# Input and first weights in eight pieces by feature, the RMS factor applied at evacuation, and an output projection by feature, in a hybrid attention layer

## What is computed

```
xn = x * rsqrt(mean(x*x) + eps) * norm_g          # x: (544 tokens, 1024 features)
h  = xn @ w_in                                    # one projection, 6728 columns
qa, ka, va, ua, qi, ki, wi, qb, kb, vb, ub, ga, gb = split(h)
# A: indexer scores relu(qi . ki) weighted by wi, top-k keys, softmax attention (8 heads of 64)
# B: stick-breaking attention (8 heads of 64)
ya = (A * silu(ua)) @ w_a_out ; yb = (B * silu(ub)) @ w_b_out
y  = x + (sigmoid(ga) * ya + sigmoid(gb) * yb) @ w_o
# outputs: y, and the new rows of ka, va, ki, kb, vb for prompt and sample
```

## Time and profile before

| | us |
|---|---|
| median of 3 runs (lowest to highest) | 618.91 (618.16 to 620.35) |
| the profiled execution, its own time | 619.36 |
| its span, first to last instruction | 617.6 |
| PE busy in the span | 585.4 (95%) |
| DVE / ACT / POOL busy | 328.4 / 259.2 / 92.5 |
| share of PE in the chain that ended last | 90% |
| mean granted TensorE clock | 0.981 |

### The profile page before, as it was taken

How to read it: one execution, slowest core, us unless ns; L and a number is a source line. 1 busy time by engine, 2 the same in 40 slices (tenths; PEclk the granted TensorE clock), 3 DMA queues, 4 the chain that set the end, 5 groups by cost and what they waited for, 6 DMA issues and landing times.

```text
span 617.6 us, 10710 instructions
## 1 busy us (share of the span) xinstructions
PE 585.4 (95%) x4582; PEld 548.7 (89%) x4582; DVE 328.4 (53%) x619; ACT 259.2 (42%) x398; POOL 92.5 (15%) x82
## 2 busy tenths in 40 slices
PE   4699999999999999999989999995999999999998
PEld 3699999998887888878979898885999999999997
DVE  3614546688787786646764566447244322245331
ACT  5332545544587667740263455544122212213110
POOL 3701000300131325420600000150000000000000
PEclk9799999999999999998999999986999999999999
DMA  8532214062022020002542210210333322345411
GB/s 243 176 106 70 79 62 148 2 208 70 2 69 69 2 68 1 1 1 85 193 152 68 70 35 2 69 36 0 103 103 88 84 62 76 103 137 190 153 46 39
DMA packets 58176, 50.48 MB, mean 82 GB/s; under 512 B 4304, under 2 KB 53840, under 8 KB 58128
## 3 DMA queue, kind: packets, MB, share of 16 engines
q1 hardware_dynamic: 58128, 49.79, 26.2%
HBM read 42.82 MB, written 6.82 MB: 80 GB/s over the span
## 4 chain that ended last, share of the span: by engine, by line
PE 90%; ACT 4%; DVE 2%; DMA 1%; issue 1%; POOL 1%; SPq 0%; DVEq 0%; ACTq 0%
PE PS L518 36%; PE PS L789 15%; PE PS L840 8%; PE PS L857 7%; PE PS L502 3%; PE PS L668 3%; PE PS L610 3%; PE PS L640 2%; PE PS L580 2%; PE PS L723 2%; PE PS L767 2%; PE PS L746 1%; DMA tm<-in_x_prompt 1%; PE PS L645 1%; PE PS L861 1%
## 5 line engine op out<-in xcount | busy, mean ns | idle before, releaser
L1183 DVE TENSOR_TENSOR wlo<-raw,whi 128x2048 fp32r<-128x2048 f32 (+2 forms) x39 | 79.6, 2042 | 111.1 <-ACT whi L908 110.7
L518 PE MATMUL PS<-whi,xhi 128*128 128x256 f32 x384 | 110.6, 288 | 2.5 <-ACT q_flat L938 1.1
L518 PE MATMUL PS<-wlo,xhi 128*128 128x256 f32 x384 | 109.1, 284 | 0.0
L518 PE MATMUL PS<-whi,xlo 128*128 128x256 f32 x384 | 108.6, 283 | 0.0
L518 PEld LDWEIGHTS PS<-whi,xhi 128*128 128x128 f32 x384 | 73.1, 190 | 4.7 <-ACT q_flat L938 1.3
L789 PE MATMUL PS<-xhi,whi 128*128 128x272 f32 x256 | 74.6, 291 | 0.0
L789 PE MATMUL PS<-xlo,whi 128*128 128x272 f32 x256 | 74.5, 291 | 0.0
L789 PE MATMUL PS<-xhi,wlo 128*128 128x272 f32 x256 | 74.4, 290 | 0.0
L518 PEld LDWEIGHTS PS<-whi,xlo 128*128 128x128 f32 x384 | 73.3, 191 | 0.0
L518 PEld LDWEIGHTS PS<-wlo,xhi 128*128 128x128 f32 x384 | 72.9, 190 | 0.0
L518 PE MATMUL PS<-xhi,whi 128*128 128x272 f32 (+1 forms) x208 | 62.4, 300 | 4.8 <-POOL xlo L1622 3.4
(11 more groups left out here) (213 smaller groups left out, 1239.6 us busy)
## 6 DMA issues: line engine op xcount, KB each, us to landing
raw<-in_w_in SPq DMA_DIRECT2D x18, 1024.0 KB, 5.2
raw<-in_w_in SPq DMA_DIRECT2D x16, 512.0 KB, 4.5
raw<-in_w_o SPq DMA_DIRECT2D x4, 1024.0 KB, 6.2
tm<-in_x_prompt SPq DMA_DIRECT2D x4, 512.0 KB, 6.6
out<-vals SPq DMA_DIRECT2D x2, 1024.0 KB, 4.3
out<-tm SPq DMA_DIRECT2D x2, 1024.0 KB, 7.6
raw<-in_w_a_out SPq DMA_DIRECT2D x8, 256.0 KB, 3.0
raw<-in_w_b_out SPq DMA_DIRECT2D x8, 256.0 KB, 3.3
```

The costliest lines, as they stand in the source:

```text
L518: mm = pe.matmul(out, lhsT, rhs, start=(k == 0), stop=(k == 23))
L1183: dve.tensor_tensor(wlo[:, uu % 2, 0:n], raw[:, uu % 2, 0:n], whi[:, uu % 2, 0:n].bitcast(F32), ALU.subtract).then_inc(w_lo, 1)
```

## The change

- x comes feature-major, and piece c (128 partitions by 1128 columns: 544 tokens, the 72 `kw` columns and the 512 `qi` columns) is one load, eight in all (`x_kw_qi`). The array is laid out ahead of the launch, and so are the other weights (`w_units`, `w_mixes`), where a unit is now one contiguous block.
- For each piece ACT makes `xhi` (with `norm_g` as the scale), `fhi` (weights) and the squares; DVE makes `xlo`, `flo` and the running sum `x_sum`. PE then accumulates `kw` in banks 6 and 7 and all of `qi` in banks 0 to 4, piece after piece. The transposes of x are gone.
- The inverse root of the mean square is no longer applied to x. In piece 7 PE sums `x_sum` over the partitions (five matmuls with two columns); DVE, then POOL make `xrs`. ACT applies it as the scale of the copies of token-major groups. For feature-major groups it is spread over all partitions (`rB`: POOL widens it, PE transposes with five matmuls inside `vb0`, DVE copies). A feature-major group is multiplied by `rB` on DVE: the `qb` groups (`query_out`, ACT did them before), all `u` groups (`u_scaled`, ACT did half), and the gates, before ACT's sigmoid.
- On DVE `query_out` stands between the rounds of top-k.
- The rotations of 512 prompt rows are done in two halves.
- The output projection is feature-major: 8 feature tiles by 2 halves of 272 tokens, 16 groups of 24 matmuls, and y is stored feature-major (`y_fm`).

```diff
-UNITS = [("kw", "kw"), ("qi0", "tm"), ("qi1", "tm"), ("vb0", "tm"), ("vb1", "tm"), ("kb0", "tm"),
+FIRST = KW + W
+CHUNK_COLS = NT + FIRST
+UNITS = [("vb0", "tm"), ("vb1", "tm"), ("kb0", "tm"),
          ("kb1", "tm"), ("qb0", "fm"), ("qb1", "fm"), ("ka0", "tm"), ("ka1", "tm"), ("qa0", "tm"),
...
+            sp.dma_start(gx, norm_g).then_inc(gx_in, 16)
+            for c in range(KC):
+                sp.dma_start(stage(c), x_kw_qi[c]).then_inc(x_in[c], 16)
             load_unit(0)
...
+            for c in range(KC):
+                pe.wait_ge(x_lo, c + 1)
+                pe.wait_ge(f_lo, c + 1)
+                fpart = (fhi, flo)
+                for h in range(2):
+                    for k, (a, b) in enumerate(PASSES):
+                        mm = pe.matmul(ps[0:KW, 6 + h, 0:HALF_NT], fpart[b][:, c, 0:KW],
+                                       xpart[a][:, c, HALF_NT * h:HALF_NT * (h + 1)],
+                                       start=(c + k == 0), stop=(c == KC - 1 and k == 2))
+                    if c == KC - 1:
+                        mm.then_inc(kw_done, 1)
+                for t, (t0, n) in enumerate(TILES[0:4]):
+                    for k, (a, b) in enumerate(PASSES):
+                        mm = pe.matmul(ps[:, t, :], xpart[a][:, c, t0:t0 + n], fpart[b][:, c, KW:FIRST],
+                                       start=(c + k == 0), stop=(c == KC - 1 and k == 2))
+                    if c == KC - 1:
+                        mm.then_inc(qi_done, 1)
+                    if c == KC - 1 and t == 0:
+                        pe.wait_ge(const_ready, 3)
+                        pe.wait_ge(x_added, KC)
+                        for tt in range(5):
+                            s0, m = (P * tt, P) if tt < 4 else (SEQ, 2 * DEC)
+                            ss = pe.matmul(ps[0:m, 5, 2 * tt:2 * tt + 2], x_sum[:, s0:s0 + m], unity,
+                                           start=True, stop=True)
+                        ss.then_inc(x_ss, 1)
+                pe.wait_ge(x_st, c + 1)
+                for b in range(2):
+                    mm = pe.matmul(ps[0:2 * DEC, 4, :], xst[:, c, :], fpart[b][:, c, KW:FIRST],
+                                   start=(c + b == 0), stop=(c == KC - 1 and b == 1))
+            mm.then_inc(qi_done, 1)
...
-            for g in range(FIRST_GROUP[U["qi0"]] + 1, LAST_GROUP[U["qi0"]] + 1):
+            for g in range(2):
                 group(g)
-            unit("qi1")
-            unit("vb0")
+            pe.wait_ge(r_wide_ready, 1)
+            pe.wait_ge(qi_out, 5)
+            for t, (t0, n) in enumerate(TILES):
+                last = pe.matmul(flat[:, 1536 + t0:1536 + t0 + n], r_wide[0:n, t, :], ident[0:n, 0:n], start=True, stop=True)
+            last.then_inc(rb_done, 1)
+            for g in range(2, LAST_GROUP[U["vb0"]] + 1):
+                group(g)
...
-                    pe.wait_ge(gates_sig, d)
+                    pe.wait_ge(gates_out, 2 * d)
...
-                t0, n = TILES[t]
+                e, h = divmod(g, 2)
+                uu = N_PROJ + 2 * (D // P) + e // 2
...
+                    for a, b in PASSES:
+                        mm = pe.matmul(ps[:, g % 8, 0:HALF_NT], wview(wpart[b], uu)[:, c, P * (e % 2):P * (e % 2) + P],
+                                       mpart[a][:, c, HALF_NT * h:HALF_NT * (h + 1)],
+                                       start=(c + a + b == 0), stop=(c == KC - 1 and a == 1))
...
+            act.wait_ge(gx_in, 16)
+            for c in range(KC):
+                act.wait_ge(x_in[c], 16)
+                act.activation(xhi[:, c, :], stage(c)[:, 0:NT], ACT.Copy, scale=gx[:, c:c + 1]).then_inc(x_hi, 1)
+                act.activation(fhi[:, c, :], stage(c)[:, NT:CHUNK_COLS], ACT.Copy).then_inc(f_hi, 1)
+                if c >= 4:
+                    act.wait_ge(x_added, c - 3)
+                act.activation(x_square[:, c % 4, :], stage(c)[:, 0:NT], ACT.Square).then_inc(x_sq, 1)
+            w_high(0)
+            w_high(1)
...
+            act.wait_ge(x_rs, 1)
...
+                act.wait_ge(qi_done, t + 1)
+                if t == 4:
+                    act.activation(qi_low, ps[DEC:2 * DEC, 4, :], ACT.Copy, scale=xrs[DEC:2 * DEC, 4:5])
+                act.activation(tm[0:n, t, 0:W], ps[0:n, t, :], ACT.Copy, scale=xrs[0:n, t:t + 1]).then_inc(qi_out, 1)
+                if t == 3:
+                    act.wait_ge(kw_tr, 1)
+                    for tt, (t0, n) in enumerate(TILES):
+                        last = act.activation(tm[0:n, tt, W:W + KW], ps[0:n, 5, KW * tt:KW * tt + KW], ACT.Copy,
+                                              scale=xrs[0:n, tt:tt + 1])
+                    last.then_inc(kw_out, 1)
...
+                ins = act.activation(dst, bank[0:n, 0:UC], ACT.Copy, scale=xrs[0:n, t:t + 1])
...
+            for c in range(KC):
+                dve.wait_ge(x_hi, c + 1)
+                dve.scalar_tensor_tensor(xlo[:, c, :], stage(c)[:, 0:NT], gx[:, c:c + 1], xhi[:, c, :].bitcast(F32),
+                                         ALU.mult, ALU.subtract).then_inc(x_lo, 1)
+                dve.wait_ge(f_hi, c + 1)
+                dve.tensor_tensor(flo[:, c, :], stage(c)[:, NT:CHUNK_COLS], fhi[:, c, :].bitcast(F32),
+                                  ALU.subtract).then_inc(f_lo, 1)
+                dve.wait_ge(x_sq, c + 1)
+                if c == 0:
+                    dve.tensor_copy(x_sum[:, 0:NT], x_square[:, 0, :]).then_inc(x_added, 1)
+                else:
+                    dve.wait_ge(x_added, c)
+                    last = dve.tensor_tensor(x_sum[:, 0:NT], x_sum[:, 0:NT], x_square[:, c % 4, :], ALU.add)
+                    if c < KC - 1:
+                        last.then_inc(x_added, 1)
+            link(last)
+            dve.tensor_copy(x_sum[:, NT:NT + DEC], x_sum[:, SEQ:NT]).then_inc(x_added, 1)
...
+            w_low(1)
+            dve.wait_ge(x_ss, 1)
+            dve.tensor_scalar(xss[:, 0:4], ps[:, 5, 0:8:2], 1.0 / D, EPS, ALU.mult, ALU.add)
+            dve.tensor_scalar(xss[0:2 * DEC, 4:5], ps[0:2 * DEC, 5, 8:9], 1.0 / D, EPS, ALU.mult, ALU.add).then_inc(x_mean, 1)
...
-            for uu in (7, 8):
-                w_low(uu)
-                for _ in range(9 - uu):
+            def query_out(g):
+
+                dve.wait_ge(group_done, g + 1)
+                (f, h), bank = GROUPS[g][1], ps[:, BANK[g], :]
+                p = 2 * int(UNITS[GROUPS[g][0]][0][2]) + f
+                c1 = min(HALF_NT * (h + 1), SEQ) - HALF_NT * h
+                for r, hh in ((0, 2 * p), (HD, 2 * p + 1)):
+                    ins = dve.scalar_tensor_tensor(qT[r:r + HD, hh, HALF_NT * h:HALF_NT * h + c1], bank[r:r + HD, 0:c1],
+                                                   HD ** -0.5, r_half(h)[r:r + HD, 0:c1], ALU.mult, ALU.mult)
+                    if c1 < HALF_NT:
+                        ins = dve.scalar_tensor_tensor(qS[r:r + HD, hh, :], bank[r:r + HD, c1:HALF_NT], HD ** -0.5,
+                                                       r_half(h)[r:r + HD, c1:HALF_NT], ALU.mult, ALU.mult)
+                ins.then_inc(group_out, 1)
+
+            w_low(U["qb0"])
+            w_low(U["qb1"])
+            topk_round(next(rounds))
+            for k in range(4):
+                query_out(FIRST_GROUP[U["qb0"]] + k)
+                if k % 2:
                     topk_round(next(rounds))
             for n in B_ITEMS:
                 item(n)
-            w_low(9)
-            for _ in range(4):
+            w_low(U["ka0"])
+            for k in range(4):
+                query_out(FIRST_GROUP[U["qb1"]] + k)
                 topk_round(next(rounds))
...
+            def u_scaled(g):
+
+                u_tile, bank = u_group(g)
+                dve.wait_ge(group_done, g + 1)
+                dve.tensor_tensor(u_tile, bank, r_half(GROUPS[g][1][1]), ALU.mult).then_inc(group_out, 1)
...
-                for n in u_groups(t):
-                    if n % 2 == 0:
-                        u_tile, bank = u_group(g0 + n)
-                        dve.wait_ge(group_done, g0 + n + 1)
-                        dve.tensor_copy(u_tile, bank).then_inc(group_out, 1)
+                mine = u_groups(t)
+                if mine:
+                    u_scaled(g0 + mine[0])
                 if t < N_STEPS:
                     normed(t)
+                if len(mine) > 1:
+                    u_scaled(g0 + mine[1])
...
+                if d == 0:
+                    dve.wait_ge(o_lo, 4)
+                else:
+                    dve.wait_ge(mixed, d)
+                for f in range(2):
+                    dve.wait_ge(gates_done, 2 * d + f + 1)
+                    dve.tensor_tensor(sg[:, f, :].rearrange("p (a n) -> p a n", a=2), ps[:, 2 * f:2 * f + 2, 0:HALF_NT],
+                                      rB.rearrange("p (a n) -> p a n", a=2), ALU.mult).then_inc(gates_out, 1)
...
-            add_sample("qi0")
+            pool.wait_ge(x_mean, 1)
+            pool.tensor_tensor(xrs[:, 0:4], xss[:, 0:4], halves[:, 0:4], ALU.pow)
```

(6 more changed lines are left out.)

410 lines of the change are left out of this document (148 added, 262 removed).

## The result

| | before | changed |
|---|---|---|
| median (lowest to highest) | 619.6 (618.16 to 620.35), 4 runs | 626.69 (626.08 to 627.63), 4 runs |
| ratio to before, 95% interval | | 1.0113 (1.0091 to 1.0134) |
| profiled execution, its own time / span | 619.36 / 617.6 | 626.47 / 624.7 |

The changed kernel is 1.1% slower, 7.1 us. (One further run of before makes its median 619.6; the forecast started from the 618.91 of three.) The prediction was 615.5 with a range of 609.5 to 620.5: wrong in sign and outside its range. The page has PE busy for less time than in the earlier trace rows, DVE for more.

The account below looks back on a forecast made before the run. PE, busy 95% of the span, was taken as the bound. Head -15.0, output projection -4.7, tail -0.5, query stage +14.6 and clock recovery +2.2 sum to -3.4 us: 615.5 us from a median of 618.91, range 609.5 to 620.5.

Parts of the forecast that it names:

- Costs set to nothing: Copies on ACT, u groups on DVE, the gates' multiplications and larger weight loads were claimed to add no time.
- the forecast's own sign of being wrong: Prediction wrong if PE waits for a third thing of several us, or if DVE's rounds leave no wait.
- the head's term of -15.0: From the start to vb1: PE starts at 7.3, vb1 at 59.1 instead of 74.12, -15.0 us, bounds -13 and -16.
- a rival at 0.08: Head: the first pieces run at half clock and cost 1.8 us, giving 617.3; chance 0.08.
- The query stage: qb0 to ka0: PE waits for DVE's query copies behind top-k rounds, 3.6 and 6.5 us; ka0 starts 14.6 us later.
- the rival that it stays up: Query stage: the waits come but PE's clock stays full, giving 611.7; chance 0.14.
- The recovery's +2.2: Behind the wait before ka0: PE's clock recovers from half, costing 2.2 us.
- The output projection: Last stage: 384 matmuls of 272 columns take 48.2 us instead of 52.9, -4.7 us.
- The tail: Behind the last matmul: one DVE addition instead of two, -0.5 us.
- ACT's scaled copies: Token-major groups: ACT's copies with a scale were claimed to cost what the plain copies did, no extra time.
- The rival on slow pieces: Head: pieces arrive slower than 145 GB/s and PE waits for each, +6.6 us at 120 GB/s, giving 622.1; chance 0.03.
- (b): End of attention steps, named after the result: DVE's order lets POOL start beside the normalization, 4.7 us; no forecast term.

Follow-up runs that it names:

- e1_pool_waits: Changed kernel with POOL starting its products only after DVE has normalized the last softmax step: 623.14 us, ratio 1.0055.
- e8_norm_first: Changed kernel with DVE, at the last softmax step, normalizing first and scaling the last u group after it: 622.98 us, ratio 1.0051.
- c1_before_collide: Kernel before with one wait added: at the last softmax step DVE normalizes only once all u groups are copied out: 624.39 us, ratio 1.0069.
- e3_table_first: Changed kernel with one tiny ACT copy ahead of its wait for the first piece, so the activation table loads earlier: 627.06 us, ratio 1.0117.
- e4_warm: e3_table_first with sixteen fp32 matmuls of 128 x 128 on PE ahead of piece 0: 624.25 us, ratio 1.0075.
- e2_copies_first: Changed kernel with DVE's top-k rounds moved so that query copies stand behind fewer of them, four rounds going behind the copies and later: 612.21 us, ratio 0.9887.
- e6_all: Changed kernel with the edits of e1_pool_waits, e2_copies_first and e3_table_first together: 607.32 us, ratio 0.9801.
- e5_act_copies: Changed kernel with the qb query copies back on ACT, without the factor rB, rounds left in place: 613.31 us, ratio 0.9901.

## Why the prediction was wrong

- **The step that failed first: "Costs set to nothing".** Of the `u` groups it said that DVE "copies a group before it normalizes; PE has several us of other groups before it needs either". It asked what PE waits for, and not what the copy releases. `group_out` of the last `u` group is what POOL's products wait for, so moving that copy from ACT to DVE, ahead of the normalization, moved POOL's start beside it. Nor is it true at the last step that PE has other groups left: the chain goes from the last `u` group to L1496 and on to the gates. Cost 4.7 us, shown by e1_pool_waits, e8_norm_first and c1_before_collide: 166.2, 166.3 and 171.0 us for the stage, against 171.0 in the changed kernel. No rival named it; the forecast's own sign of being wrong, a wait of PE for a third thing of several us, did come, at L765.
- **The second: the head's term of -15.0, which was -10.8.** The 4.2 us are 1.8 of later start and the half pace. The start: the piece landed at 5.4 (1.24 + 4.12 in the chain) and not 4.9, and 1.28 us of table load came behind it; in the kernel before the table load ran at 0.79, ahead of any data. e3_table_first shows the start at 7.59 without it. The half pace: 3.5 us in this run, so 1.7 lost. The term had counted 1.8 us of half clock as "not paid again"; it was paid again, in the first pieces. What is left, about 0.7, is small: `vb0` with the matmuls for `rB` took 14.7 for 14.4 and ended at 59.07, the items took 4.3 for 4.1 (two scaled copies), and the pieces 4.00 for 3.97 each.
- The half pace was a rival at 0.08, and was set aside for a wrong reason. The forecast took the transposes of the earlier trace rows (eight in 1.94, 0.24 each) with the granted clock of 1.00 in the earlier trace rows as full speed. But the same transposes of 128 x 128 in the items of attention B, later in that trace, start 0.11 us apart, sixteen of them from 136.62 to 138.36:

```profile
136.62 1.91 PE L552 MATMUL PS<-ident,tm 128*128 128x128 f32 x16
```

So the early ones ran at half. The column reads 1.00 at 9.2 to 12.2 as well, where the matmuls' distance shows half; in the head it can't be relied on. The Trainium skill's rule in "TensorE: Matmul & The Clock Gate" (Part 1, the HAM clock gate), that throttled is the default and activity releases it, was right, and e4_warm agrees with it: 0.23 us from the first piece after 6 us of other matmuls, where e3_table_first took 0.43. The prediction's "this trace disagrees" was a misreading.
- **The query stage was right**, in mechanism and size: +15.8 against +14.6, with waits of 3.8 and 6.5 against 3.6 and 6.5. The 1.2 us come in small pieces: DVE's low part of `qb1` ended 0.3 later than forecast, the later rounds took 3.86 from start to next copy instead of 3.75, five times, and the first group of `qb1` ran at half pace (4.74 us) and ended 0.2 us behind the low part of `ka0`, on which the forecast had put the path. The clock fell behind both waits, so the rival that it stays up is out. The recovery's +2.2 looks exact in the table, and that is luck in part: 1.8 us of it are there by the third group of the `ka` units (10.8 us after `ka0` started, 9.0 before; the first took 4.80 instead of 3.09), and 0.4 came later, between 265 and 326 us, half of it in two scaled copies of ACT (see below).
- **The output projection was right**: 384 matmuls in 48.31 us against 48.2. The tail saved 0.2, not 0.5.
- Pieces came 4.0 us apart at full pace, the bandwidth was no limit (418 GB/s in the stretch above), and the gates' multiplications and `i_rows` cost nothing, as said. The forecast put ACT's scaled copies at no extra cost too; they took 0.47 or 0.48 us for 256 columns against 0.38 or 0.39, which shows where they stand in the chain: two in the items of the head and two at 276 and 287 us, 0.1 each. The rival on slow pieces is out.
- The size of the error: with (b) and the head at their measured values the forecast's sum of -3.4 becomes +5.5, so the two account for 8.9 of 10.5 us. e1_pool_waits, which mends (b) alone, still lies above the range at 623.14; both had to be known.

Where the gain went: the head and the output projection gave 15.4 us, and DVE's order in two places took 22.7 (15.8 with 2.2 behind it, most of that clock, and 4.7). e2_copies_first and e1_pool_waits give back 14.5 and 3.6, and the sum, e6_all, shows the change at -2%.

## What to carry to other kernels

When work moves from one engine to another, follow every semaphore that it signals, and ask who is released by it and what that one will run beside, not only who waits for the data. A copy that PE waits for must not stand behind a round of work that nobody waits for; order the queue of a shared engine by who is waiting. And PE that has done nothing starts at half pace: read it from the distance of the matmuls' starts, and spend the wait for the first load on matmuls into a bank that is free.

## What the runs showed of the hardware

- **DVE and POOL in turn.** Two scalings of 128 x 288 (fp32, SBUF to SBUF) took 2.58 and 2.63 us each when POOL's product of 128 x 1088 had started 0.03 us before, and 2.50 and 2.58 in c1_before_collide, against 0.65 for both alone. POOL's two took 4.98 together, 2.49 each: each scaling ended about when one product of POOL did. The low part beside POOL (two SBUF sources, 1.21 alone) took 2.50 in e1_pool_waits, 1.67 in e8_norm_first and 1.62 before, having started 1.1, 1.9 and 2.0 us into POOL's first product. In all three it ended 1.1 us after that product did, and POOL's second product took 3.51, 3.51 and 3.52 instead of 2.53. So these two took turns as well, each waiting for the other: the later DVE starts, the shorter its own wait. The Trainium skill, page "SBUF — State Buffer", section "Who interferes with whom", says that a `tensor_scalar` in a two-port mode and an instruction of GpSimd exclude each other for their whole length, and that the one that starts first wins. The scalings agree with it: each ended within 0.2 us of the end of a product that had started before it.
- **The half pace at the start varies.** It lasted 3.0 to 6.1 us over seven traces, and so the head's time moved by 1.4 us in kernels with the same head. A single trace can't price the head to better than that.
- **The granted clock of the head.** The profile gives 1.00 before and during the first pieces while 512 columns took 0.43 us; at 126 to 128 us it gives 0.50 where the pace is half too.
- **Half clock without a wait.** In or behind a stretch of small matmuls (48 of 32 columns, L677 before, L692 after) the clock falls in all seven traces looked at there: it reads 0.50 at 290 to 292 us before, at 296 to 298 in the changed kernel and at 282 to 286 in e2_copies_first, where it had come to 0.56 at 280 to 282 with PE busy for all of the 2 us. e5_act_copies has a second fall at 268 to 270, and its eight matmuls of L683 took 3.99 us instead of 2.30. From `ka0` to the last `u` group e5_act_copies took 245.0 us against 241.7 before, most of the difference in these two places.
